# Loading the second expert matrices of the last quad by expert instead of in four pieces

## What is computed

```
def expert_block(args):
    xb, e = args
    a = jax.nn.silu(xb @ w1[e]) * (xb @ w3[e])
    return a @ w2[e]
```

## Time and profile before

| | |
|---|---|
| median of three runs | 1631.07 us (1630.53 to 1631.41) |
| the profiled execution: its own time, its span | 1631.4 us, 1629.6 us |
| TensorE products busy | 1492.6 us, 92% |
| VectorE, ScalarE busy | 765.4 us, 319.1 us |
| DMA queue of SyncE | 369.60 MB, 59.3% of 16 engines over the span |
| mean granted clock of TensorE | 0.96 of full |
| experts of quads 1 to 7 | about 1234 to 1625 us of the span |

### The profile page before, as it was taken

One profiled execution on the slowest core, in us unless ns is written; L12 is line 12 of the kernel. 1 busy time (PEld: TensorE's weight loads), 2 busy tenths in 40 slices (PEclk: granted clock), 3 DMA queues, 4 the chain that ended last, 5 costly groups with the idle time before them and its releaser, 6 DMA issues.

```text
span 1629.6 us, 20177 instructions
## 1 busy us (share of the span) xinstructions
PE 1492.6 (92%) x8400; PEld 1036.6 (64%) x8400; DVE 765.4 (47%) x1467; ACT 319.1 (20%) x653; POOL 22.7 (1%) x41
## 2 busy tenths in 40 slices
PE   8999999999999999999999999999998577566578
PEld 5687889899544788899999445755564133133132
DVE  3647666766756647665766665644331000000001
ACT  2234422122001125421122001334410000000000
POOL 0000000000000000000000001200000000000000
PEclk9999999999999999999999999999999787788789
DMA  8547134445442634224454455745689999999997
GB/s 306 191 159 253 56 104 155 155 156 178 184 155 89 220 127 153 78 81 157 163 188 163 157 197 176 251 152 210 258 320 427 427 427 427 427 428 427 426 420 307
DMA packets 106253, 380.28 MB, mean 233 GB/s; under 512 B 6261, under 2 KB 16629, under 8 KB 95473
## 3 DMA queue, kind: packets, MB, share of 16 engines
q1 hardware_dynamic: 103280, 369.60, 59.3%
q0 software_dynamic: 2880, 9.36, 2.0%
HBM read 377.31 MB, written 5.73 MB: 235 GB/s over the span
## 4 chain that ended last, share of the span: by engine, by line
PE 77%; DMA 17%; DVE 3%; SPq 1%; issue 1%; ACT 1%; DVEq 0%; ACTq 0%
DMA ring<-in_w 17%; PE bank L1446 12%; PE bank L1492 12%; PE bank L1107 10%; PE bank L1114 8%; PE bank L1272 5%; PE bank L1632 4%; PE bank L1246 3%; PE bank L1222 2%; PE bank L1198 2%; PE bank L1389 2%; PE bank L1541 2%; PE bank L1657 1%; PE bank L1419 1%; PE bank L1421 1%; PE bank L1150 1%
## 5 line engine op out<-in xcount | busy, mean ns | idle before, releaser
L1107 PE MATMUL bank<-hT,ring 128*128 128x256 f32 x832 | 186.7, 381 | 0.0
L1107 PEld LDWEIGHTS bank<-hT,ring 128*128 128x128 f32 x832 | 155.5, 190 | 24.1 <-issue 3.4
L1632 PE MATMUL bank<-ring,region 128*32 128x512 f32 x208 | 118.3, 734 | 51.0 <-DMA region<-in_w 51.0
L1632 PE MATMUL bank<-region 128*32 128x512 f32 x512 | 118.5, 735 | 49.6 <-DMA ring<-in_w 49.6
L1492 PE MATMUL bank<-region 128*128 128x512 f32 x320 | 140.6, 592 | 0.0
L1492 PEld LDWEIGHTS bank<-region 128*128 128x128 f32 x320 | 60.5, 190 | 74.6 <-issue 74.6
L1446 PE MATMUL bank<-region 128*128 128x128 f32 x768 | 100.5, 275 | 0.0
L1446 PEld LDWEIGHTS bank<-region 128*128 128x128 f32 x768 | 93.0, 192 | 0.0
L1632 PEld LDWEIGHTS bank<-region 128*32 128x32 f32 x512 | 29.4, 131 | 95.0 <-issue 95.0
L1632 PEld LDWEIGHTS bank<-ring,region 128*32 128x32 f32 x208 | 26.1, 131 | 86.7 <-issue 86.7
L1114 PE MATMUL bank<-ring,region 128*128 128x512 f32 (+2 forms) x224 | 72.2, 479 | 2.7 <-ACT region L1772 1.4
(11 more groups left out here) (467 smaller groups left out, 2497.4 us busy)
## 6 DMA issues: line engine op xcount, KB each, us to landing
region<-in_w SPq DMA_DIRECT2D x48, 2048.0 KB, 35.9
ring<-in_w SPq DMA_DIRECT2D x31, 2048.0 KB, 39.3
ring<-in_w_in SPq DMA_DIRECT2D x27, 2048.0 KB, 8.0
ring<-in_w_up SPq DMA_DIRECT2D x16, 2048.0 KB, 8.2
ring<-in_w_down SPq DMA_DIRECT2D x32, 1024.0 KB, 6.2
own_slot<-in_w SPq DMA_DIRECT2D x8, 2048.0 KB, 43.1
ring<-in_w_out SPq DMA_DIRECT2D x6, 2048.0 KB, 7.9
ring<-in_w_in SPq DMA_DIRECT2D x6, 1536.0 KB, 7.3
```

The source lines that it names most:

```text
L1107: t = mm(b[:, 0:T], w[:, k, :], act[:, k, :], start=(k == 0), stop=(k == KD - 1))
L1632: t = mm(b[32 * e:32 * e + 32, :], xg[:, k, 32 * e:32 * e + 32], four[e][c][:, 512 * (k % 2):512 * (k % 2) + 512], start=(k == 0), stop=(k ...
```

## The change

In `by_expert` the last quad's exception begins at group 2 instead of group 1, and the fillers between second-matrix pieces go with the pieces:

```diff
@@ -552,7 +552,7 @@
         def by_expert(q, g):
 
-            return q > 0 and not (q == QUADS - 1 and g > 0)
+            return q > 0 and not (q == QUADS - 1 and g > 1)
 
@@ -1648,9 +1648,6 @@
                         if by_expert(q, j):
                             quad_up(q, j, b, c)
                             continue
-                        if q == QUADS - 1 and j == 1 and c:
-                            for _ in range(3):
-                                mm(psum[1][:, :], ident, x[:, 0, 0:512], start=True, stop=True)
                         w = expert_chunk(QCH * q + 4 * j + c)
```

## The result

| | before | changed |
|---|---|---|
| median of 22 executions each | 1630.82 us | 1633.38 us |
| lowest and highest | 1630.22, 1632.38 us | 1631.77, 1636.06 us |
| ratio of the changed kernel to the one before | | 1.0016 [1.0010, 1.0022] |
| profiled execution: its own time, its span | 1631.4, 1629.6 us | 1631.77, 1630.0 us |

The change makes the kernel 0.16% slower, 2.6 us. That is inside the 0.2% that I had called no change, and its interval, 1.6 to 3.6 us, is well clear of zero. The spread in this comparison is larger too: 2.2 us before, 4.3 us now. The profiled execution is the fastest of the 22, only 0.4 us slower than the profiled one before, so its trace shows how the change works but not all of the 2.6 us.

The account below looks back on a forecast made before the run. TensorE and the load stream were taken to run side by side to the end; 1.7 us for the products' place plus 2.1 us for the low clock gave +3.8 us, 1634.9 us, range 1632.3 to 1636.3.

Parts of the forecast that it names:

- What bounds the end: Quad 7: TensorE and the load stream run side by side to the end, TensorE a few us behind.
- When the joint products start: Quad 7's second-matrix products wait for all four chunks and start at 1598.42, 19.58 us after its first product.
- split price: Loading quad 7's four second-matrix chunks at the split layout's 409 GB/s, landing 0.9 us later than at the whole layout's rate.
- third rival: Quad 7's second matrices load no faster whole: landing at 1599.2, sum +4.7, 1635.8 us; chance 0.08.
- How long they take: Quad 7's joint products start at the low clock after idling; 9.34 us to VectorE's multiplication, which starts 3.8 us later.
- It moves by the same amount if it runs at the same clock.: Everything behind VectorE's multiplication, 20.7 us to the scatter's end, shifts by the same +3.8 us.
- first rival: Clock stays up over the turns between second- and third-matrix stages: 1.7 us come back, +2.1, 1633.2 us; chance 0.27.
- second case: The clock stays up over the turns, as in the first rival: +1.3 to +2.8 us; chance 0.27.
- forecast's own range: Low clock after the joint wait and after the turns: +3.0 to +4.5, 1634.1 to 1635.6 us; chance 0.58.
- The two terms: Of 3.8 us, 1.7 from all products standing behind the last chunk, 2.1 from part of them at the low clock.
- The case that I had put at 0: Clock also survives the 10 us joint wait and stays up over the turns: sum 0, about 1631 us; chance 0.04.
- No load is met: Third-matrix chunks land up to 0.9 us earlier, are wanted 3.8 us later; no wait appears, the 0.49 us one goes.

Follow-up runs that it names:

- e1: Kernel before without its three fillers between quad 7's second-matrix pieces, matrices still in pieces: 1630.32 us, before 1630.70.
- e8: Kernel before without any of its five fillers in quad 7, second and third matrices still in pieces: 1630.99 us, before 1631.30.
- e10: Kernel before with one identity product before and one behind quad 7's four turns: 1630.96 us, before 1631.21.
- e7: Changed kernel, ten identity products in the joint wait, one each side of the turns, one instead of three in both third-matrix places: 1630.12 us, before 1631.30.
- e6: Changed kernel with quad 7's third matrices also whole by expert, last chunk in one load, no third-matrix fillers: 1637.50 us, before 1631.30.
- e2: Changed kernel with ten identity products between the turn of the puts and quad 7's joint wait: 1630.99 us, before 1630.70.
- e3: Changed kernel with one identity product before and one behind quad 7's four turns: 1633.29 us, before 1630.70.
- e5: Changed kernel without the two fillers between the third-matrix pieces: 1630.32 us, before 1631.30.
- e4: Changed kernel with ten identity products in the joint wait and one before and one behind the turns: 1631.05 us, before 1630.70.
- e11: Same kernel as e7, timed once more in another comparison: 1629.77 us, before 1631.21.
- e9: Like e7 but with no identity product in the two third-matrix places: 1630.06 us, before 1631.21.

## Why the prediction was right, and where it was off

**What bounds the end.** Right. The kernel before runs beside its stream of loads, and taking its fillers out saves no time: e1 and e8 removed 8.3 and 13.9 us of them for nothing, and e10 showed that a gain on TensorE turns into a wait for the last load.

**When the joint products start.** Right to 0.06 us (1598.36 for 1598.42). The split price, my upper end and the third rival, did not come: the spacing of 19.6 us of the quads before held in this kernel and in seven of the eight later profiles with whole second matrices; only e7 has 19.9. The 19.2 us that I had estimated beside it from the bytes alone were 0.4 us too few (19.60 were measured).

**How long they take.** Right as a mean. I took 9.34 us to VectorE's multiplication; in the four profiled executions that wait unfilled it was 8.51, 9.52 (1598.83 to 1608.35), 9.67 and 9.73 us (e6, 1598.33 to 1608.06). The wait for the fourth chunk lowers the clock in all four, and e2 shows what that costs: 2.3 us of the 2.6 went with the fillers in the wait.

**"It moves by the same amount if it runs at the same clock."** Here the size went wrong: 2.6 us and not 3.8, and 1633.38 us and not 1634.9. The 3.8 us hold only if the clock is low over the turns as well, and I put that at 0.58. In the profiled execution it was not: the first third-matrix piece took 1.92 us and not 3.55, the tail from VectorE to the end of the scatter 19.0 us and not 20.7, and the scatter ended at 1625.86 and not at 1628.5. That a tail shorter than 19 us would mean the first rival stands in the prediction. e3 points the same way for the median: with the gap filled the difference is 2.6 us as well, though its interval, 0.5 to 3.4 us, leaves room for a part of the low piece. The sum of the second case alone was +2.1 us, 1633.2 us, and the median lies 0.2 us from it. So the first rival is probably the larger part of the result, and the chances of the two cases should have been the other way round. By their times alone, 8 of the 22 executions lie in the forecast's own range or above it (from 1634.1 us up) and 14 below, but that does not show what each of them did. The profiled one (1631.77, +0.4 us) is below both cases. Its scatter ended 1.2 us later, near the second case's lower end of +1.3, and 0.8 us of that went again behind the scatter, where the profiled execution before, to which I had added, took longest of all (5.0 us).

I had argued from one row, the kernel before in quad 7, that the gap of two idle spells and four turns lowers the clock, and held against the other quads that they had a longer busy stretch before it. Behind a joint run that had begun at the low clock the gap left it up (the changed kernel, e5); where TensorE had stayed at the full clock from before 1590 us up to the gap it fell (the kernel before 3.55 us, e1 3.27, e8 3.41, e2 3.38). That orders these six profiles, but it is not shown as a rule: in the earlier trace rows it fell in quad 3, behind a joint run that had begun low.

**The two terms.** I had split the 3.8 us into 1.7 for the place of the products and 2.1 for the clock. At VectorE both are there: e2, without the clock's part, starts it at 1605.70, 1.8 us later than the earlier trace rows. In e2's median only 0.3 us of the 1.8 are left. The case that I had put at 0 (full clock in the joint run and over the turns) would account for its faster group; that is not shown.

**No load is met.** Right (none behind 1598.3), and it is the step from which I could have drawn more. I wrote that the third-matrix fillers "now guard a wait that is not there", and went no further; e5 shows that these 5.5 us are what passes the lateness on to the end. The loss needs both, the slow joint run and the fillers behind it: e2 takes the first away, e5 the second, and each alone takes it to within the noise.

**The range and the chances.** 1633.38 us lies in the range, which was 4 us wide because it took in the second case too. The distance of 0.16% is the case "same", to which I gave 0.35, while I gave "slower" 0.63; nothing was faster. So the direction and the range are right, and the case inside the range that I held likeliest is not the one that came.

**Left open.** Why the clock falls over the turns in some executions and not in others was not settled, and an execution without profile can only be sorted by its time. The changed kernel's slow executions, up to 1636.06 us, were not profiled.

## What to carry to other kernels

Before a filler or a small piece is removed from the last stage of a kernel that is fed by a full DMA queue, ask not what it costs but when the loads behind it land: in pieces the products ran beside the loads, whole they all stand behind the last chunk (e6: +6.2 us where nothing followed, +2.6 us where a stage followed, 0 where that stage had no fillers of its own). Fillers downstream that used to guard waits should go with the waits, since they pass every lateness on (e5: -1.0 us against the kernel before, within the noise). A filler in the wait that was made longer also took most of the loss away (e2: +0.3 us), but with the fillers downstream gone it brought nothing more that could be measured (e7 against e5: 0.2 us).

## What the runs showed of the hardware that was not expected

One program's executions differ by more than the change under study: the changed kernel's 22 executions cover 4.3 us, e2's fall into two groups, and even the kernel before covered 4.2 us in 33 executions on another chip. The clock is one source of it (the unfilled joint run took 8.51 to 9.73 us to VectorE in four profiles). Two others are of like size in the thirteen profiled executions: quad 7's first product came at 1577.9 to 1579.2 us, and 3.9 to 5.0 us passed behind the scatter. An idle time of 2.04 us behind 8.75 us of fillers was followed by a fall of the clock in the second row (e4), while 0.79, 1.18, 1.48 and 1.58 us in e2, e7, e11 and e9 left the first rows at 0.59 us. The length of the idle time alone does not order these: in e8 one of 3.20 us left the piece behind it at 1.92 us, the full clock, and one of 3.19 us some 15 us later was followed by products of 1.07 us each, the low one. The layout of a 2 MiB load went with its speed on a full queue, 409 to 410 GB/s with packets of 4 KiB against 422 to 429 with packets of 16 KiB; over the four second-matrix chunks that is 0.9 us.
